# Streaming encoder step on one core: rounding order and norm sums in the first five feed-forward tiles

## The reference

```python
x = x + g1 * y                                   # y: output of the mixer
h = rmsnorm(x, norm_ffn[l]) * (1.0 + sc2) + sh2
x = x + g2 * swiglu(h, w_up[l], w_down[l])

def swiglu(h, w_up, w_down):
    gate, up = jnp.split(h @ w_up, 2, axis=-1)
    return (jax.nn.silu(gate) * up) @ w_down
```

## Time and profile before

| | |
|---|---|
| median of 3 runs | 958.35 us (956.68 to 959.63) |
| the profiled execution | 958.35 us, span of its trace 956.5 us |
| TensorE busy | 926.9 us, 97% of the span |
| TensorE weight loads | 894.9 us, 94% |
| VectorE busy | 664.8 us, 70% |
| ScalarE busy | 434.5 us, 45% |
| GpSimd busy | 104.3 us, 11% |
| TensorE idle before line L2136, of which behind `w_lo` | 5.4 us, 4.4 us |

### The profile page before, as it was taken

The page is one execution under the profiler, slowest core; times in us unless marked ns, Lnnn a source line. Parts: engine busy times, 40 slices in busy tenths (PEclk is TensorE's granted clock), DMA queues, the critical chain, the costliest instruction groups (busy, mean ns, idle before and its releaser), DMA issues.

```text
span 956.5 us, 22427 instructions
## 1 busy us (share of the span) xinstructions
PE 926.9 (97%) x9441; PEld 894.9 (94%) x9441; DVE 664.8 (70%) x1248; ACT 434.5 (45%) x800; POOL 104.3 (11%) x131
## 2 busy tenths in 40 slices
PE   5999999999999999999999999889999999999997
PEld 5899898999999999999999999889999999999997
DVE  3678879866667676487667876789434899994453
ACT  6587445424324444542322256456313566652213
POOL 0100011112120010100100000123001222220000
PEclk9999999999999999999999999999999999999999
DMA  9824233444333332316643232232223333323222
GB/s 350 260 75 146 59 97 111 123 117 123 111 110 112 109 83 59 111 56 208 173 121 101 85 96 74 66 89 73 84 83 116 89 117 105 89 78 100 66 67 94
DMA packets 146174, 104.88 MB, mean 110 GB/s; under 512 B 5169, under 2 KB 138999, under 8 KB 144923
## 3 DMA queue, kind: packets, MB, share of 16 engines
q1 hardware_dynamic: 139099, 79.23, 28.3%
q0 software_dynamic: 6352, 22.00, 7.5%
q10 hardware_dynamic: 624, 2.23, 0.6%
HBM read 100.12 MB, written 3.31 MB: 108 GB/s over the span
## 4 chain that ended last, share of the span: by engine, by line
PE 50%; DVE 3%; ACT 2%; issue 2%; POOL 0%; ACTq 0%; POOLq 0%; DVEq 0%
PE G L2136 31%; PE G L2226 18%; ACT w_hi L1201 1%; DVE w_lo L1574 1%; POOL w_sum L1146 0%; PE R L2147 0%; DVE x_lo L1663 0%; DVE val L2098 0%; DVE x L1657 0%; DVE x L1654 0%; DVE a_near L1583 0%; DVE sq L2081 0%; PE R L2270 0%; PE R L2144 0%; DVE val L2089 0%
## 5 line engine op out<-in xcount | busy, mean ns | idle before, releaser
L2136 PE MATMUL G<-h_hi,w_hi 128*128 128x272 f32 (+1 forms) x912 | 273.2, 300 | 5.4 <-DVE w_lo L1574 4.4
L2136 PE MATMUL G<-h_lo,w_hi 128*128 128x272 f32 (+1 forms) x912 | 263.0, 288 | 0.0
L2136 PE MATMUL G<-h_hi,w_lo 128*128 128x272 f32 (+1 forms) x912 | 262.8, 288 | 0.0
L1574 DVE TENSOR_TENSOR w_lo<-raw,w_hi 128x1024 fp32r<-128x1024 f32 (+2 forms) x113 | 119.1, 1054 | 114.2 <-ACT w_hi L1201 113.4
L2136 PEld LDWEIGHTS G<-h_hi,w_hi 128*128 128x128 f32 x912 | 171.9, 188 | 9.2 <-issue 5.2
L2136 PEld LDWEIGHTS G<-h_lo,w_hi 128*128 128x128 f32 x912 | 172.1, 189 | 0.1
L2136 PEld LDWEIGHTS G<-h_hi,w_lo 128*128 128x128 f32 x912 | 171.7, 188 | 0.0
L1201 ACT ACTIVATE w_hi<-raw 128x1024 fp32r<-128x1024 f32 (+2 forms) x113 | 103.5, 915 | 89.3 <-PE G L2136 89.1
L1146 POOL TENSOR_TENSOR w_sum<-raw 128x512 f32<-128x512 f32 x34 | 48.7, 1433 | 326.6 <-DMA raw<-in_w_up 188.0
L2226 PE MATMUL G<-x_hi,sum_hi 128*128 128x272 f32 x272 | 79.0, 290 | 1.6 <-ACT partial L1304 1.6
L2226 PE MATMUL G<-x_hi,sum_lo 128*128 128x272 f32 x272 | 78.7, 290 | 0.0
(11 more groups left out here) (328 smaller groups left out, 2056.5 us busy)
## 6 DMA issues: line engine op xcount, KB each, us to landing
raw<-in_w_in SPq DMA_DIRECT2D x48, 512.0 KB, 4.0
raw<-in_w_up SPq DMA_DIRECT2D x44, 512.0 KB, 3.9
w_ada<-in_w_ada_t POOLq DMA_DIRECT2D x49, 256.0 KB, 3.1
wada<-in_w_ada_s SPq DMA_DIRECT2D x8, 1024.0 KB, 14.1
raw<-in_w_down SPq DMA_DIRECT2D x16, 320.0 KB, 3.1
raw<-in_w_out SPq DMA_DIRECT2D x8, 512.0 KB, 4.1
raw<-in_w_down SPq DMA_DIRECT2D x8, 512.0 KB, 4.2
w_ada_t<-in_w_ada_t POOLq DMA_DIRECT2D x15, 256.0 KB, 3.2
```

Of the source, the lines that this page charges most:

```text
L1574: dve.tensor_tensor(lo, raw[:, i % RAW, 0:job.nk, 0:job.m], hi.bitcast(F32), ALU.subtract).then_inc(w_lo_done, 1)
L2136: ins = pe.matmul(out, w, x, start=(job.first and k == 0 and p == 0), stop=(job.last and k == job.nk - 1 and p == 2))
```

## The change

`SUMS_AT` goes from 4 to 2, so each tile of the first pair does two chunks ahead of the norm sums and six behind them. All four `x_norm`, two `x_shift` and the first `x_sum` now stand ahead of the rest of the first pair, in the order B11, B12, NT1, B22 as the diff has it. The plan of the ten plain tiles is written out anew: behind tile i come, in this order, `split_hi` of tile i + 2, the evacuation of tile i, `split_lo` of tile i + 2, and then the rest of the work for that place (table `rest`). The multiplications `up_mul` move into that table. The sums of the first unit are spread over the places behind ffu3, ffg4 and ffu4; before, they stood behind ffu4's products together with the rounding of tiles. In `prepare` and `FIRST_LO` (both runs of units) the rest of sum 2 is taken ahead of that of "g". Which engine makes which sum (`SUM_BY`) is not changed: GpSimd has sums 1 and 3, VectorE 2 and 4, as before.

```diff
-FIRST_LO = (1, "g", 2, 4, 3, "d")
+FIRST_LO = (1, 2, "g", 4, 3, "d")
-SUMS_AT = 4
+SUMS_AT = 2
...
-        return [("q_add", u, 1), ("q_add", u, 2), ("q_hi", u, 1), ("q_lo", u, 1), ("q_hi", u, 2), ("q_add", u, 4)], \
-               [("q_hi", u, "g"), ("q_lo", u, "g"), ("q_lo", u, 2), ("q_hi", u, 4), ("q_add", u, 3)], \
+        return [("q_add", u, 1), ("q_hi", u, 1), ("q_add", u, 2), ("q_lo", u, 1), ("q_hi", u, 2), ("q_add", u, 4)], \
+               [("q_hi", u, "g"), ("q_lo", u, 2), ("q_lo", u, "g"), ("q_hi", u, 4), ("q_add", u, 3)], \
...
-    for b in NORMED[:3]:
+    for b in NORMED:
         do("x_norm", b)
-    do("x_shift", B11)
+    for b in (B11, B12):
+        do("x_shift", b)
+    do("x_sum", NT1)
+    do("x_shift", B22)
...
-    behind_step(("half", first + 3), ("x_sum", T3), ("x_lo", NT1), ("x_hi", B22), ("x_sum", T4), ("x_hi", NT2))
-    behind_step(("half", first + 4), ("x_lo", B22), ("x_hi", T3))
-    behind_step(("half", first + 5), ("x_lo", NT2), ("x_hi", B21), ("x_lo", T3))
-    behind_step(("half", first + 6), ("x_hi", T4), ("x_lo", B21))
-    sums, high, low = prepare(0)
-    behind_step(("half", last), ("x_lo", T4), *sums, *high)
-    plan.extend(low)
...
+    rest[1] = [("x_sum", NT2), ("x_hi", B11), ("up_mul", 0)]
+    rest[2] = [("x_shift", B21), ("x_hi", NT1), ("x_lo", B11), ("x_hi", B22), ("x_sum", T3)]
+    rest[3] = [("x_hi", NT2), ("up_mul", 1), ("x_sum", T4), ("x_lo", NT1), ("x_hi", T3)]
+    rest[4] = [("x_hi", B21), ("x_lo", B22), ("x_lo", NT2), ("x_hi", T4)]
+    rest[5] = [("up_mul", 2), ("x_lo", T3), ("x_lo", B21)]
+    rest[6] = [("x_lo", T4)]
+    sums, high, low = prepare(0)
+    rest[7] = [("up_mul", 3), *sums]
+    rest[8] = high
+    rest[9] = [low[0], ("up_mul", 4), *low[1:]]
...
+        ahead = n > 1 and n + 2 < len(evac)
+        if ahead:
+            plan.append(("split_hi", i))
+        plan.append(one)
+        if n + 2 < len(evac):
+            plan.append(("split_lo", i))
+        plan.extend(rest[n])
```

More of the change, by code:

```diff
@@ L418, in make_plan @@
     do("sums")
-    for b in NORMED[:3]:
+    for b in NORMED:
         do("x_norm", b)
-    do("x_shift", B11)
+    for b in (B11, B12):
+        do("x_shift", b)
+    do("x_sum", NT1)
+    do("x_shift", B22)
+    mark = len(plan)
     duo(lambda: up(0))
@@ L424, in make_plan @@
         up(m)
[L425 to L431, removed]
-    behind_step(("half", first + 3), ("x_sum", T3), ("x_lo", NT1), ("x_hi", B22), ("x_sum", T4), ("x_hi", NT2))
-    behind_step(("half", first + 4), ("x_lo", B22), ("x_hi", T3))
-    behind_step(("half", first + 5), ("x_lo", NT2), ("x_hi", B21), ("x_lo", T3))
-    behind_step(("half", first + 6), ("x_hi", T4), ("x_lo", B21))
-    sums, high, low = prepare(0)
-    behind_step(("half", last), ("x_lo", T4), *sums, *high)
-    plan.extend(low)
+    evac = [s for s in plan[mark:] if s[0] == "evac"]
+    rest = {n: [] for n in range(len(evac))}
+    rest[1] = [("x_sum", NT2), ("x_hi", B11), ("up_mul", 0)]
[4 more added lines that the diff above has]
+    rest[6] = [("x_lo", T4)]
+    sums, high, low = prepare(0)
+    rest[7] = [("up_mul", 3), *sums]
+    rest[8] = high
+    rest[9] = [low[0], ("up_mul", 4), *low[1:]]
+    del plan[mark:]
+    plan.append(("duo", u0, u0 + 1))
+    for n, one in enumerate(evac):
+        i = u0 + n + 2
+        if n >= 2:
+            plan.extend([("job", u0 + n), ("half", u0 + n)])
+        if n == 0:
+            plan.append(("split_hi", i + 1))
+            plan.append(one)
+            continue
+        ahead = n > 1 and n + 2 < len(evac)
+        if ahead:
+            plan.append(("split_hi", i))
+        plan.append(one)
+        if n + 2 < len(evac):
+            plan.append(("split_lo", i))
+        plan.extend(rest[n])
     quick_run(range(PLAIN, PART))
```

## The result

The changed kernel took 950.87 us (median of 7 runs, 950.15 to 954.05), the kernel before, on the same chip in the same rounds, 958.35 us (7 runs, 956.3 to 960.51). The ratio is 0.9934 with a 95% interval of 0.992 to 0.9949: **faster by 0.5 to 0.8%**, about 6.3 us. The profiled execution took 952.0 us against 958.35, with a span of 950.2 us against 956.5. The forecast was 952.0 us.

The account below looks back on a forecast made before the run. TensorE, busy nearly throughout, was taken as the bound, so only its idle stretches could be won. 5.3 us in the plain tiles became 4.9 at product 2 and 6.4 at product 6: 958.35 - 6.4, called 952.0 us, range 950.6 to 955.6.

Parts of the forecast that it names:

- Scale: Plain tiles ffg2 to ffu4: six tiles without a wait put unit 0's product 0 at 618.3; at most 5.3 us to win.
- Part 1, cost nothing: First pair: moving the norm sums behind two chunks costs TensorE nothing; the pair still ends at about 569.2.
- Part 1, `rn`: Norm factor on ScalarE: Ln starts right behind its table load, so the first `x_norm` comes 2.84 us earlier.
- Rival 2: First evacuation late because Ln starts later than its table load's end: up to 954.5 or 955.9 us; chance 0.14.
- Part 2, 0.3 us to spare: Ahead of the first evacuation: NT1 ends 0.3 us before ffg0's evacuation; without early sums ffg1 starts about 2.5 us later.
- Part 3, both `w_lo` waits go: Plain tiles: rounding ahead of evacuation has `w_lo` ready 2.2 us after a tile's end; behind up tiles VectorE needs 5.95 of 6.07.
- Part 4, the meeting is absorbed: GpSimd's two first sums, at about 601.9, meet VectorE's work; even the whole 2.3 us costs TensorE nothing.
- Part 5, product 2: Unit 0: product 2 starts at 622.9, its wait growing from 0.95 to about 1.5 us; gain 4.9 us.
- Part 5, product 6: Unit 0: VectorE's sum 4 starts 0.3 us before GpSimd's sum, winning the race; product 6 at 629.2, gain 6.4 us.
- Rival 1: GpSimd wins the race for sum 4, product 6 keeps its old distance from product 2: 953.4 us; chance 0.30.
- The rest, unit 1 on unchanged: From unit 1 on, locked to TensorE's own products, the lead is carried through unchanged; swapped rests worth nothing.
- Rival 4: Slower: unit 0's 1.57 us wait returns in the 16 later units, up to 978 us; chance 0.04.

Follow-up runs that it names:

- experiment 2: The kernel before with only SUMS_AT = 2 (norm sums behind two chunks): 959.7 us, ratio 0.9998.
- experiment 1: The changed kernel with SUMS_AT back at 4 (norm sums behind four chunks): 954.29 us, ratio 0.9967.
- experiment 5: The kernel before with the new plan order and swapped rests, but sums behind four chunks and blocks about where they were: 952.09 us, ratio 0.9934.
- experiment 6: The kernel before with GpSimd's two first sums waiting until `w_lo` of ffu4 is made: 955.94 us, one execution.
- experiment 7: The changed kernel with the last `up_mul` ahead of the rest of sum 4 on VectorE: 951.35 us, one execution.
- experiment 4: The changed kernel with VectorE's sum 4 of unit 1 waiting for GpSimd's sum 3: 955.92 us, one execution.
- experiment 3: The kernel before with GpSimd's sum 3 of unit 1 waiting for VectorE's sum 4: 957.77 us, one execution.
- experiment 12: The changed kernel measured again with nothing edited: 951.48 us, ratio 0.9935.
- 9: The kernel of experiment 5 with GpSimd's sum 3 of unit 1 waiting for VectorE's sum 4: 950.62 us, ratio 0.9923.

## Why the prediction was right, point by point

- **Scale.** Right. Six tiles without a wait: ffg2 to product 0 was reckoned, and ffg1 to product 0 fell by 5.28 us where 5.3 was the most there was.
- **Part 1, cost nothing.** Off by 0.2 us. Experiment 2 has it alone: chunk to ffg1 14.86 instead of 14.65. ffu0 is now due 12 matmuls earlier than before, and its accumulator, that of the last tile of the stage before, is still being emptied. TensorE and VectorE of the changed kernel:

```profile
556.95 0.40 PE L2155 MATMUL G<-h_hi,up_hi 128*128 128x272 f32 x1
```

```profile
555.86 1.03 DVE L2075 SCALAR_TENSOR_TENSOR xT<-G,mod,xT 128x272 f32<-128x272 f32 x3
```

  Twelve matmuls of 0.126 us behind 555.33 end at 556.84; the row on VectorE that empties the accumulator ends at 556.89, and ffu0 starts right behind it. The view of that row's line names TensorE's weight load as waiting for it, 0.2 us. Before, four chunks of ffg0 covered that until 557.98. I had named the square as the thing that could be late and did not ask who held the accumulator.
- **Part 1, `rn`.** Right. The first `x_norm` was to be 2.84 us earlier; measured from the first chunk it came 9.62 us before (564.57 - 554.95) and 6.80 now (562.13 - 555.33): 2.82 us earlier. On ScalarE Ln stood directly behind the load of its table:

```profile
559.22 1.28 ACT L1197 ACT_TABLE_LOAD   x1
560.55 0.86 ACT L1248 ACTIVATE rn<-R,eps 128x512 f32<-128x512 f32 x2
```

  The load ends at 560.50 and Ln starts at 560.55. The drain of about 1.38 us that the Trainium skill has ("ScalarE: Activation LUTs", What ACT_TABLE_LOAD costs) is not seen here either. Rival 2 needed it, and did not happen.
- **Part 2, 0.3 us to spare.** Right (0.40). The price without Part 1 was right for ffg1 (about 2.5 us forecast, 2.54 in experiment 1) and too low for the whole: the stretch at the lower clock behind the wait cost 1.55 us more, a term that my sum did not have.
- **Part 3, both `w_lo` waits go.** Right, and experiment 5 shows that the order does it. The tight place behind an up tile held.
- **Part 4, the meeting is absorbed.** Right: `x_lo` 2.36 us, no wait. GpSimd's sums came at 601.04 where I had 601.9: they followed the `w_lo` of ffu3 by 3.9 us (its row is 595.94 and 1.23 us) and not by 5.6, so that distance was mis-sized, within what the cover could take. Experiment 6 shows that the meeting made the slow `x_lo` before, and that removing it alone would have moved the wait on.
- **Part 5, product 2.** 622.9 forecast; 623.36 is 622.8 once the 0.38 us of the later start and the 0.21 of Part 1 are taken off. Its wait was 1.29 instead of 1.5: the rest of sum 4 cost 0.48 us where I had 0.6 (experiment 7, and 4.28 us from the evacuation at 619.08 to product 2 instead of 3.80).
- **Part 5, product 6.** 629.2 forecast; 629.83 less the same 0.59 is 629.2. The race was won by 0.24 us where I had 0.3. Rival 1 was real: experiment 4 makes GpSimd first and costs 1.67 us (I had 1.5), and experiment 7 lets it be first by 0.03 us. The rule of the Trainium skill ("SBUF — State Buffer", SBUF: two separate sides), that the one that starts first keeps the port, agrees with the rows of the changed kernel and of experiments 3 and 7: 0.68 or 0.69 us when VectorE is first, 1.81 when it starts 0.03 us second.
- **The rest, unit 1 on unchanged.** Off by 0.4 us, on the good side. Before, TensorE waited 0.38 us in unit 1 for a copy. GpSimd and VectorE there, before:

```profile
640.60 2.22 POOL L1146 TENSOR_TENSOR w_sum<-raw 128x512 f32<-128x512 f32 x1 [6.54 <-PE G L2226]
```

```profile
640.45 1.23 DVE L1683 TENSOR_TENSOR w_lo<-raw,w_hi 128x1024 fp32r<-128x1024 f32 x1 [0.51 <-ACT w_hi L1288]
...
642.96 0.69 DVE L1674 TENSOR_TENSOR w_sum<-w_sum,raw 128x512 f32<-128x512 f32 x1 [1.28 <-POOL w_sum L1146]
```

  After:

```profile
634.77 1.29 POOL L1165 TENSOR_TENSOR w_sum<-raw 128x512 f32<-128x512 f32 x1 [4.85 <-PE G L2245]
```

```profile
635.24 1.90 DVE L1702 TENSOR_TENSOR w_lo<-raw,w_hi 128x1024 fp32r<-128x1024 f32 x1 [0.50 <-ACT w_hi L1307]
```

  It is a second race of the same kind, and here GpSimd should be first, since VectorE's next sum waits for GpSimd's (1.28 us before, no idle time after). GpSimd starts 4.95 us behind product 6 before and 4.94 after, VectorE with its `w_lo` 4.80 us before and 5.41 after, where product 6 came early. In all fourteen traces the wait is there when GpSimd was first at sum 4 and gone when VectorE was. I took unit 1 as locked to TensorE's products and did not read its own 0.38 us. Rival 4, the later units out of step, did not happen.
- **Sum.** 6.4 us forecast, 6.3 between the spans and 6.3 by the ratio: -0.2 for Part 1, -0.4 for the later start, +0.4 for unit 1 and some small terms cancel. The start's 0.38 us lies ahead of all that the change touches: the first chunk stands anywhere from 552.98 to 557.25 in the fourteen traces, and at 554.00 in the changed kernel's second one. So it is luck that the spans agree with the forecast to 0.1 us and that the profiled execution took just the 952.0 forecast; what bears the forecast out are the distances in the trace, which repeat to 0.01 us (experiment 12). That the two medians are 7.5 us apart is within what single runs scatter (up to 4 us).

## What to carry to other kernels

On engines that walk a list in order, put what the next tile waits for (here the rounding of its weights) ahead of the clearing up of the last one, and everything else behind it: that order gave 5.5 of 6.2 us without removing an instruction. Where GpSimd and VectorE both read on-chip memory at about the same time, look at who starts first: a few hundredths of a microsecond decided over one us, and a wait of two lines can settle it (60.55 to 59.42 us at product 6 from experiment 5 to 9, too little to be seen in the total). Work put ahead of the first evacuation was free here only with an earlier start of its inputs, so such a pair of edits must be judged together.

## What the runs showed of the hardware that I had not expected

**Idle stretches of TensorE can cost twice.** Behind 2.74 us of idle time (experiment 1) and 2.37 us (experiment 6) the granted clock fell from 1.00 to 0.50, 2.4 to 1.2 GHz, and it cost another 1.55 us in the first. In experiment 3 it fell behind the 2.49 us ahead of ffu4, which the kernel before has too. Experiment 3:

```profile
617.50:619.50 2.00, 2.00 (x13) 2.00 (x12) 2.00 (x5) 0.00 (x0) 0.00 (x0) 0.60 0.50 150
```

Before, behind the same wait:

```profile
618.00:620.00 2.00, 2.00 (x18) 2.00 (x17) 2.00 (x5) 1.17 (x3) 0.00 (x0) 1.00 0.76 228
```

From ffu4 to product 0 it took 7.17 us before and 7.69 in experiment 3, and this although the wait of 0.87 us that stood ahead of product 0 was filled by the slow matmuls. So the same wait of 2.49 us cost half a microsecond more in this trace; in the profile of before and in that of experiment 2 it did not. The changed kernel has no wait of that length in this stage. Whether this is part of the scatter between runs was not measured.

**The second waits for the whole instruction of the first, on either side.** A 128x512 sum on VectorE took 0.68 or 0.69 us started first, 1.81 started 0.03 us second; GpSimd's, 1.29 first and up to 2.22 second. In experiment 7 GpSimd's row ended at 627.03 and VectorE's at 627.58, 0.55 us later: about one addition, so VectorE did next to nothing until GpSimd was through. In all these rows the loss is with the one that came second.
